# Pooling stage of a two-layer decoder step: small products of the sample outputs placed behind the third gate unit

## The chip, the cores and the metric

The kernel runs on one core of one Trainium2 chip. The metric is the time of one execution on the device in microseconds (us). The engines have in-order programs that meet at semaphores: TensorE (matmuls, which write to PSUM), VectorE, ScalarE, GpSimd, and SyncE (SP), which issues most of the DMAs.

## The reference

One inference step of a decoder trunk with two layers, for a prompt group of 1024 tokens and a sample group of 8 sequences with one new token each, which share all weights. So T = 1032 token columns go through each layer. What matters here:

```
m = pool_mix(v_ext, pos_out)          # 4 groups of 128 channels, windows 2, 4, 8, 16
y = einsum('btgc,gcd->btgd', m, pool_w)            # one 128x128 product for each group
pool = y * pool_scale * silu(gate)                 # gate: 4 groups of x @ w_in
b_pool = pool @ pool_up
b_attn = (o * silu(ag)) @ attn_up                  # o: attention output
sub = (sigmoid(mg_pool) * b_pool + sigmoid(mg_attn) * b_attn) @ w_out
```

For the sample group the attention output is `o = einsum('bthc,chd->bthd', o_lat, w_uv)`, with 8 tokens, 8 heads and a latent of 256.

## The kernel before

Activations lie transposed: channels on the 128 partitions, 1032 tokens along the free dimension. Every large product is a **unit** (lines 604 to 620): a slab of weights of 128 output channels, multiplied as three products of split fp32 numbers (high x high, high x low, low x high), each in three parts of 344 columns. A gate unit has 8 weight tiles, so 72 matmuls; a mix unit has one tile, so 9. A unit writes to one of two sets of three PSUM banks, in turn (bank set 0 and 1, `unit_free[0]` and `unit_free[1]`), and waits until the unit before the last, in the same set, has been read. Weights come by DMA into a ring of four pieces (`RAW`), and GpSimd splits each piece into `WH` and `WL` (lines 512 and 514).

The stage at hand is written out by hand, once for each of the two layers. TensorE (lines 943 to 972) goes through: gate unit 0, a small transpose, gate unit 1, 32 small products for the sample outputs (line 952), four transposes (line 956), mix unit 0, 16 **small products** of the sample outputs with `UVF` (line 963, semaphore `os_done`), gate unit 2, mix unit 1, gate unit 3, mix units 2 and 3, and then the loop of the merge units (line 976), which begins with products of `OGH` and `OGL`.

ScalarE (lines 1296 to 1319) takes its work in this order: copies MXH 0 and 1; evacuation of gate units 0 and 1 (`pool_gate`: a copy to SPGB, line 1282, and a sigmoid to SGB, line 1283, which frees the bank set); PVO and its two DMAs; product copy 0 (PMH); a wait for `os_done` (line 1308); copies MXH 2 and 3; a wait for `s_done`; four copies OGH from OT; evacuation of gate unit 2; product copy 1; evacuation of gate unit 3; product copies 2 and 3.

VectorE (lines 1772 to 1803): pooling means 0 and 1 (`mixed`, line 1722: running sums by doubling, into MXF, which ScalarE copies to MXH and VectorE takes the low part MXL from); the sample weights; `gated(0)`, mean 2, `gated(1)`; OLT from line 952's products; the pooling product 0 (line 1762) and PML (line 1770); a wait for `os_done` (line 1790); OT of the sample columns (line 1794, `s_done`); MXL 2; mean 3; MXL 3; pooling product 1; `gated(2)`, `gated(3)`; pooling products 2 and 3.

GpSimd splits weights throughout. Behind mix unit 1 and the OGH copies it makes four OGL (line 561), two behind the split of mix unit 2's weights and two behind that of mix unit 3's, and then splits the merge units' weights.

Copies of ScalarE are recorded on line 1047, where their helper stands.

Of the kernel before, what the change touches and what calls it, by code (L numbers as in the profile page):

```python
# [93 lines left out]
def slab_of(name, n):  # L94

    return next(s for s, x in enumerate(SLABS) if x[0:2] == (name, n))
# [41 lines left out]
def build(nc, x_all, wstream, pages, page_table, ple, state, ukt, uvf, gains, lng, lnb, table, ident,  # L138
          mask, inv, y_all, lat_p, rope_p, pool_p, lat_s, rope_s, pool_s):
    with ExitStack() as ctx:  # L140
# [201 lines left out]

        BLOCKS = [(h, j) for h in range(2) for j in range(SEQ // P)]
        SECOND = [sum(j >= 4 for _, j in BLOCKS[:n]) for n in range(17)]
        GROUPS = SEQ // P
        O_BANK, FILL_BANK = 5, 2
# [226 lines left out]
        def _(pe):  # L573
# [30 lines left out]
            def unit(l, s, xh, xl, i=0, per=0, between=None):  # L604

                par, kt, tiles = par_of(s), SLABS[s][2], piece_tiles(s)
                pe.wait_ge(unit_free[par], q_of(l, s, i, per) + 1)
                for j in range(SLABS[s][3]):
                    slot, q = piece_of(l, s, j, i, per)
                    pe.wait_ge(w_split[slot], q + 1)  # L610
                    for k in range(tiles * j, tiles * (j + 1)):
                        at = slice((k - tiles * j) * P, (k - tiles * j + 1) * P)
                        for n, (w, x) in enumerate(((WH, xh), (WH, xl), (WL, xh))):
                            for c in range(3):
                                last = nc.tensor.matmul(PS[:, 3 * par + c, 0:CH], w[:, slot, at],  # L615
                                                        x(k)[:, c * CH:(c + 1) * CH], start=(k == 0 and n == 0),
                                                        stop=(k == kt - 1 and n == 2))
                    last.then_inc(w_used[slot], 1)
                    if between is not None:
                        between(j)  # L620

            def rows(tensor, base=0):
                return lambda k: tensor[:, base + k, :]
# [166 lines left out]
            for l in range(DEPTH):  # L790
# [144 lines left out]
                def gate_unit(g):  # L935
                    unit(l, slab_of("pg", g), rows(XH), rows(XL))

                def mix_unit(g):

                    pe.wait_ge(mix_ready, 4 * l + g + 1)  # L940
                    unit(l, slab_of("pw", g), lambda k: MXH[g // 2][:, g % 2, :], lambda k: MXL[g // 2][:, g % 2, :])
# [14 lines left out]
                    last = nc.tensor.transpose(PS[0:23, 6, g * P:(g + 1) * P], PVX[:, g, PAD + T - 23:PAD + T], IDENT[:])  # L956
                last.then_inc(pvt_done, 1)
                mix_unit(0)
                pe.wait_ge(aux_in, 32 * l + 32)
                pe.wait_ge(olt, l + 1)  # L960
                for h in range(PAIRS):
# [2 lines left out]
                                                UVF[:, k, h * P:(h + 1) * P],  # L964
                                                OLT[:, k, 2 * h:2 * h + 2, :], start=(k == 0), stop=(k == KC - 1))
                last.then_inc(os_done, 1)

                gate_unit(2)
                mix_unit(1)
                gate_unit(3)  # L970
                mix_unit(2)
# [476 lines left out]
        def _(dve):  # L1448
# [41 lines left out]
            def x_wait(t):  # L1490
                for i, (lo, _) in enumerate(X_LOADS):
                    if t == lo:
                        dve.wait_ge(x_in[i], 16)
# [31 lines left out]
            for l in range(DEPTH):  # L1525
# [36 lines left out]
                def scaled(part):  # L1562

                    lo, hi = ((0, KC), (KC, KQ + KC))[part]
                    dve.wait_ge(rt_ready, 6 * l + 3 * part + 3)
                    own(v.reciprocal(RT[:, 1 - part, :], RT[:, 1 - part, :]))
                    for _, k in LATENTS[lo:hi]:
                        v.scalar_tensor_tensor(out=CR[:, k, :], in0=CR[:, k, :], scalar=GL[:, k:k + 1], in1=RT[:, 1 - part, :],
                                               op0=ALU.mult, op1=ALU.mult).then_inc(cn_ready, 1)
# [469 lines left out]
```

## Time and profile before

| | us |
|---|---|
| median of 3 runs | 2044.54 |
| lowest and highest | 2037.77, 2045.38 |
| the profiled execution | 2032.2 |
| its span in the trace | 2030.4 |
| TensorE busy | 1912.3 |
| VectorE, GpSimd, ScalarE busy | 905.2, 737.0, 565.4 |
| mean granted clock of TensorE | 0.98 |

The span goes from the first to the last instruction of the profiled execution; 1.8 us of its time lie around it. All starts below are from the span's start. The pooling stage lies at about 575 to 640 us in the first layer and 1567 to 1632 us in the second. The granted clock is a share of full speed: 1.00 is 2.4 GHz and 0.50 is 1.2 GHz. Matmuls overlap, so a unit's time is read from the start of its first matmul to the start of what follows.

### The profile page before, as it was taken

How to read it: one execution, taken by the hardware profiler on the slowest of the kernel's cores; microseconds unless marked ns; L12 is line 12 of the kernel's file. 1: busy time of each engine (PE TensorE's matmuls, PEld its weight loads, DVE VectorE, ACT ScalarE, POOL GpSimd, SP SyncE). 2: the span in 40 equal slices, each digit the busy share in tenths (PEclk: the TensorE clock that was granted, in tenths of full speed). 3: DMA queues.
4: the chain of work that ended last, by engine and by line, in shares of the span. 5: the costliest groups of instructions: out<-in, count | busy, mean ns of one | idle time of the engine just before them, and what ended most of it. 6: DMA issues, size and time to landing. Idle time of an engine off the chain costs nothing.

```text
span 2030.4 us, 31146 instructions
## 1 busy us (share of the span) xinstructions
PE 1912.3 (94%) x12391; PEld 1816.3 (89%) x12391; DVE 905.2 (45%) x1484; ACT 565.4 (28%) x997; POOL 737.0 (36%) x743
## 2 busy tenths in 40 slices
PE   6999899999999999999989989999999999999994
PEld 5998888888799999999989968888878999999994
DVE  4344566664164111535454535666623721134216
ACT  6123444443122010201251334444421310120002
POOL 3332343342145333434244322343312443334434
PEclk9999999999999999999999999999999899999997
DMA  5213221053812221222132141121365122222222
GB/s 212 74 47 131 65 64 62 22 177 123 288 34 62 78 66 56 89 89 68 30 128 55 41 165 33 55 64 61 138 234 181 32 89 72 67 68 87 66 67 84
DMA packets 94746, 183.96 MB, mean 91 GB/s; under 512 B 12086, under 2 KB 35942, under 8 KB 93964
## 3 DMA queue, kind: packets, MB, share of 16 engines
q1 hardware_dynamic: 73440, 135.43, 21.7%
q10 hardware_dynamic: 21180, 46.80, 6.1%
q8 instruction: 85, 1.39, 0.3%
q14 instruction: 41, 0.34, 0.1%
HBM read 150.19 MB, written 32.45 MB: 90 GB/s over the span
## 4 chain that ended last, share of the span: by engine, by line
PE 73%; DVE 11%; ACT 9%; issue 3%; ACTq 1%; DMA 1%; POOL 1%; DVEq 0%; SPq 0%; POOLq 0%
PE PS L615 52%; PE PS L710 5%; PE PS L638 4%; PE PS L595 4%; DVE MX L1662 3%; ACT PB L1243 2%; ACT PTH L1047 2%; DVE PTL L1650 2%; PE PS L695 2%; PE PS L730 1%; PE PS L671 1%; DVE PS L1661 1%; PE PS L754 1%; DMA RAW<-in_wstream 1%; ACT FST L1047 1%
## 5 line engine op out<-in xcount | busy, mean ns | idle before, releaser
L512 POOL CAST WH<-RAW 128x512 fp32r<-128x512 f32 (+3 forms) x292 | 200.7, 687 | 905.8 <-DMA RAW<-in_wstream 905.8
L514 POOL TENSOR_TENSOR WL<-RAW,WH 128x512 fp32r<-128x512 f32 (+3 forms) x292 | 382.2, 1309 | 23.5
L615 PE MATMUL PS<-XH,WH 128*128 128x344 f32 x1344 | 290.0, 324 | 4.6 <-ACT SGB L1283 3.9
L615 PE MATMUL PS<-XL,WH 128*128 128x344 f32 x1344 | 287.4, 322 | 0.0
L615 PE MATMUL PS<-XH,WL 128*128 128x344 f32 x1344 | 286.8, 322 | 0.0
L615 PEld LDWEIGHTS PS<-XH,WH 128*128 128x128 f32 x1344 | 228.0, 190 | 7.3 <-ACT SGB L1283 4.5
L615 PEld LDWEIGHTS PS<-XH,WL 128*128 128x128 f32 x1344 | 227.5, 189 | 0.0
L615 PEld LDWEIGHTS PS<-XL,WH 128*128 128x128 f32 x1344 | 227.3, 190 | 0.0
L533 POOL TENSOR_SCALAR PB<-PB,RC 128x128 f32<-128x128 f32 (+7 forms) x128 | 96.1, 751 | 333.3 <-DVE RC L1644 333.3
L638 PE MATMUL PS<-XH,WH 128*128 128x344 f32 x384 | 127.4, 332 | 29.1 <-ACT FST L1047 29.1
L1243 ACT ACTIVATE PB<-PS,NB 128x128 f32<-128x128 f32 (+7 forms) x128 | 95.0, 742 | 188.2 <-DVE NB L1663 187.9
L1819 DVE TENSOR_TENSOR SGP<-PS,SGP 128x1032 f32<-128x1032 f32 x16 | 19.7, 1233 | 242.1 <-PE PS L615 242.1
L638 PE MATMUL PS<-XL,WH 128*128 128x344 f32 x384 | 124.3, 324 | 0.0
L638 PE MATMUL PS<-XH,WL 128*128 128x344 f32 x384 | 123.6, 322 | 0.0
L638 PEld LDWEIGHTS PS<-XH,WH 128*128 128x128 f32 x384 | 72.6, 189 | 41.1 <-ACT FST L1047 40.4
L1650 DVE TENSOR_TENSOR PTL<-PS,PTH 128x512 fp32r<-128x512 f32 (+3 forms) x128 | 75.8, 592 | 68.9 <-ACT PTH L1047 67.8
L1662 DVE TENSOR_REDUCE MX<-PS 128x1 f32<-128x128 f32 (+7 forms) x128 | 97.0, 758 | 4.4
L1047 ACT ACTIVATE PTH<-PS 128x512 fp32r<-128x512 f32 (+1 forms) x192 | 86.7, 488 | 32.1 <-PE PS L671 30.8
L660 PE MATMUL PS<-KH,QH 128*128 128x512 f32 (+1 forms) x192 | 75.4, 393 | 7.9 <-DVEq L1623 7.9
L695 PE MATMUL PS<-PTH,VSP 128*128 128x256 f32 x320 | 75.5, 272 | 3.6 <-DVE PTL L1654 3.6
L695 PE MATMUL PS<-PTL,VSP 128*128 128x256 f32 x320 | 73.8, 278 | 0.0
L638 PEld LDWEIGHTS PS<-XH,WL 128*128 128x128 f32 x384 | 72.5, 189 | 1.1
(275 smaller groups left out, 3860.2 us busy)
## 6 DMA issues: line engine op xcount, KB each, us to landing
RAW<-in_wstream SPq DMA_DIRECT2D x236, 256.0 KB, 2.7
PAGES<-in_pages SPq DMA_DIRECT2D x128, 320.0 KB, 4.9
spill_p<-PST ACTq DMA_DIRECT2D x16, 516.0 KB, 2.9
spill_g<-FST ACTq DMA_DIRECT2D x48, 172.0 KB, 1.9
SGL<-spill_g ACTq DMA_DIRECT2D x16, 516.0 KB, 4.4
PRJ<-spill_p ACTq DMA_DIRECT2D x16, 516.0 KB, 4.4
spill_v<-VSTG ACTq DMA_DIRECT2D x16, 512.0 KB, 2.8
VSP<-spill_v SPq DMA_DIRECT2D x8, 1024.0 KB, 5.3
```

The source lines that it names most:

```text
L512: pool.tensor_copy(WH[:, slot, 0:size], RAW[:, slot, 0:size]).then_inc(w_high[slot], 1)
L514: pool.tensor_tensor(WL[:, slot, 0:size], RAW[:, slot, 0:size], f(WH[:, slot, 0:size]), ALU.subtract).then_inc(w_split[slot], 1)
L533: pool.tensor_scalar(PB[:, n % 2, 0:keys], PB[:, n % 2, 0:keys], RC[:, n:n + 1], 1.0, ALU.mult, ALU.mult).then_inc(nm_done, 1)
L595: last = nc.tensor.matmul(PS[:, 3 * par + c, 0:w], wt[:, slot, at], x(k)[:, cut[c]], start=(k == 0 and n == 0), stop=(k == kt - 1 and n == 2))
L615: last = nc.tensor.matmul(PS[:, 3 * par + c, 0:CH], w[:, slot, at], x(k)[:, c * CH:(c + 1) * CH], start=(k == 0 and n == 0), stop=(k == kt ...
L638: last = nc.tensor.matmul(PS[:, FILL_BANK, 0:CH], w[:, slot, (k % 4) * P:(k % 4 + 1) * P], x[:, k, c * CH:(c + 1) * CH], start=(step == 0) ...
L695: last = nc.tensor.matmul(PS[:, o_bank(g), lo:2 * P], VSP[:, kb, h * P:(h + 1) * P], pt[:, kb, lo:2 * P], start=(kb == 0 and m == 0), stop ...
L710: last = nc.tensor.matmul(PS[:, PV_BANKS[chunk % 2], 0:CH], w[:, slot, (k % 4) * P:(k % 4 + 1) * P], x[:, k, c * CH:(c + 1) * CH], start=( ...
L1047: return nc.scalar.activation(dst, src, ACT.Copy)
L1243: nc.scalar.activation(PB[:, n % 2, 0:keys], score_banks(n)[:, 0:keys], ACT.Exp, bias=NB[:, n:n + 1], scale=SCALE, accum_out=SUM[:, n:n + ...
L1650: v.tensor_tensor(PTL[:, 0:w, c0:c0 + P], PS[:, 6, 0:w * P].rearrange("p (k c) -> p k c", c=P), f(PTH[:, 0:w, c0:c0 + P]), ALU.subtract).t ...
L1662: own(v.tensor_reduce(MX[:, n:n + 1], row[:, 0:(j + 1) * P], AX_X, ALU.max))
```

## The change

On TensorE, the call of gate unit 2 moves from behind the small products of line 963 to a place ahead of them and of the two waits in front of them. The other engines' programs stay as they are. The order becomes: mix unit 0, gate unit 2, small products, mix unit 1, gate unit 3, mix units 2 and 3.

```
                 last.then_inc(pvt_done, 1)
                 mix_unit(0)
+                gate_unit(2)
                 pe.wait_ge(aux_in, 32 * l + 32)
                 pe.wait_ge(olt, l + 1)
                 for h in range(PAIRS):
...
                 last.then_inc(os_done, 1)
-
-                gate_unit(2)
                 mix_unit(1)
                 gate_unit(3)
                 mix_unit(2)
```

## Rows read from the trace of the kernel before

**Rows 1.** The page: busy time of the engines, and the chain's shares by engine.
```profile
PE 1912.3 (94%) x12391; PEld 1816.3 (89%) x12391; DVE 905.2 (45%) x1484; ACT 565.4 (28%) x997; POOL 737.0 (36%) x743
PE 73%; DVE 11%; ACT 9%; issue 3%; ACTq 1%; DMA 1%; POOL 1%; DVEq 0%; SPq 0%; POOLq 0%
```

**Rows 2.** Waits of TensorE, 590 to 660 us: total, times, longest.
```profile
PE PS L615 <- ACT SGB L1283: 2.0, 1, 2.0
PE PS L615 <- DVEq L1766: 1.1, 1, 1.1
...
```

**Rows 3.** The chain in order of time, first layer: start, duration, what.
```profile
605.52 1.07 ACT MXH L1047
...
606.62 1.87 DVE MXL L1754
...
615.41 0.18 DVE MXF L1742
...
616.58 3.91 ACT OGH L1047 x4
...
```

**Rows 4.** Timeline of TensorE, first layer: start, duration, instructions, idle before.
```profile
583.93 0.75 PE L615 MATMUL PS<-XH,WH 128*128 128x344 f32 x3
...
595.41 3.63 PE L952 MATMUL PS<-SELW,OLS 128*128 128x8 f32 x32
598.90 0.60 PE L956 MATMUL PS<-IDENT,PVX 128*23 128x128 f32 x4
599.25 0.90 PE L615 MATMUL PS<-MXH,WH 128*128 128x344 f32 x3
...
601.92 3.56 PE L963 MATMUL PS<-OLT,UVF 128*128 128x16 f32 x16
605.33 1.21 PE L615 MATMUL PS<-XH,WH 128*128 128x344 f32 x3
...
618.82 0.64 PE L615 MATMUL PS<-MXH,WH 128*128 128x344 f32 x3
...
622.37 0.74 PE L615 MATMUL PS<-XH,WH 128*128 128x344 f32 x3 [1.97 <-ACT SGB L1283]
...
635.38 0.63 PE L615 MATMUL PS<-MXH,WH 128*128 128x344 f32 x3
```

**Rows 5.** The same timeline in the second layer.
```profile
1594.40 3.43 PE L963 MATMUL PS<-OLT,UVF 128*128 128x16 f32 x16
1597.66 1.21 PE L615 MATMUL PS<-XH,WH 128*128 128x344 f32 x3
...
1611.58 0.64 PE L615 MATMUL PS<-MXH,WH 128*128 128x344 f32 x3
...
1615.10 0.74 PE L615 MATMUL PS<-XH,WH 128*128 128x344 f32 x3 [1.93 <-ACT SGB L1283]
...
1626.59 0.63 PE L615 MATMUL PS<-MXH,WH 128*128 128x344 f32 x3
```

**Rows 6.** Windows: stretch, length, TensorE busy, granted clock, DMA share, GB/s.
```profile
605.33:609.77 4.44, 4.44 (x16) 0.50 0.00 0
...
1597.66:1602.97 5.31, 5.31 (x19) 0.50 0.00 0
```

**Rows 7.** Timeline of TensorE at the kernel's start.
```profile
14.16 1.20 PE L615 MATMUL PS<-PLH,WH 128*128 128x344 f32 x3 [6.01 <-POOL WL L514]
...
19.43 0.65 PE L615 MATMUL PS<-PLH,WH 128*128 128x344 f32 x3
```

**Rows 8.** Line 1754 alone: least, median and greatest ns; first and last start.
```profile
L1754 DVE TENSOR_TENSOR MXL<-MXF,MXH x8: 1232/1316/2245, 580.6 to 1609.4; 128x1032 fp32r<-128x1032 f32 x8
```

**Rows 9.** Timeline of VectorE, end of the third pooling mean.
```profile
600.03 0.17 DVE L1742 SCALAR_TENSOR_TENSOR MXF<-RED,PVX 128x8 f32<-128x8 f32 x1
```

**Rows 10.** Timeline of GpSimd: the first OGL pair, and weights behind the last.
```profile
621.84 5.75 POOL L561 TENSOR_TENSOR OGL<-OT,OGH 128x1032 fp32r<-128x1032 f32 x2
...
634.06 0.61 POOL L512 CAST WH<-RAW 128x512 fp32r<-128x512 f32 x1
```

More of the change, by code:

```diff
@@ L958, in _ @@
                 mix_unit(0)
+                gate_unit(2)
                 pe.wait_ge(aux_in, 32 * l + 32)
@@ L966, in _ @@
                 last.then_inc(os_done, 1)
-                gate_unit(2)
                 mix_unit(1)
```

## The prediction

> **What bounds the kernel now.** I read the page's busy shares and its chain of work first. TensorE is busy 94% of the span and holds 73% of the chain, so only two things change the time: work that TensorE does more or less slowly, and moments in which it has nothing to do [rows 1]. Next the waits of TensorE in the stretch around the change: 2.0 us for ScalarE's sigmoid (line 1283, the evacuation of gate unit 2) and 1.1 us for VectorE. The reader should see that the first is a wait of gate unit 3 for the bank set that gate unit 2 filled [rows 2]. Then the chain in order of time, followed back from that wait: gate unit 3 starts at 622.37 us, because ScalarE's two evacuations of gate unit 2 end there; these come after four copies into OGH, these after MXH, this after VectorE's fourth pooling mean (the one with window 16, to 615.6 us), this after MXL, this after another MXH copy at 605.52 us, and this after the small products of line 963 [rows 3]. So everything from 605.5 to 622.4 us, 16.9 us on ScalarE and VectorE, begins with the end of the small products (the semaphore os_done) and ends with the start of gate unit 3. It is no dependence of data for the most part: ScalarE and VectorE each have a wait for os_done in their program (lines 1308 and 1790), and what stands behind it waits too. Last, the timeline of TensorE in both layers: today gate unit 2 and mix unit 1 (13.5 + 1.6 us in layer 0) run under this chain and hide all of it but 2.0 us [rows 2, 4].
>
> **The change, part by part.** No instruction is added or removed. Gate unit 2 (72 matmuls) goes ahead of two waits and 16 small products, in each of the two layers. No DMA is issued by TensorE; SP's loads wait only for pieces that are used no later than before, so nothing is moved past SP's or GpSimd's queue.
>
> *Gate unit 2 starts earlier.* Its bank set is free (its predecessor there, gate unit 1, ends at 595.41 us, and ScalarE needs for such a set the 1.9 us from the OGH copies' end to gate unit 3's start [rows 3, 4]) and its weights are split. So it starts where mix unit 0 ends, about 601.9 and 1594.4 us, 3.4 and 3.3 us earlier [rows 4, 5].
>
> *Its duration.* A gate unit at the full clock takes 595.41 - 583.93 = 11.48 us. Gate unit 2 now takes 618.82 - 605.33 = 13.49 us in layer 0 and 1611.58 - 1597.66 = 13.92 us in layer 1 [rows 4, 5], because the granted clock was 0.50 (the 1.2 GHz level) for its first 4.44 and 5.31 us [rows 6]; 2.0 us lost in 4.44 us, so 0.45 us for each slow us. The clock had fallen after the small products of line 952, and mix unit 0 already ran slowly. It has come back 4.4 to 5.3 us after dense work began: so in rows 6, and also at the kernel's start, where the first unit began at 14.16 us after 6.01 us of idleness and was fast from 19.43 us [rows 6, 7]. With mix unit 0 directly ahead of gate unit 2, dense work begins at 599.3 us, so the clock should be back near 604.2 us, which leaves 1.6 to 2.7 slow us for gate unit 2, about 1.0 us lost: 12.5 us. Bounds: 11.5 us (never slow) and 13.9 us (as slow as today's layer 1).
>
> *The small products.* They take 605.33 - 601.92 = 3.41 us and 1597.66 - 1594.40 = 3.26 us now, at the slow clock. Behind a gate unit they would run at the full one. The nearest row is the 32 products of line 952, also with 128x128 weights and few columns, at the full clock: 598.90 - 595.41 = 3.49 us, 0.109 us each [rows 4], so 16 take 1.75 us. Bounds 1.7 and 3.4 us.
>
> *What waits behind them.* os_done thus comes 12.5 + 1.75 - 3.41 = 10.8 us later in layer 0 and 12.4 + 1.75 - 3.26 = 10.9 us later in layer 1. Queued behind its wait are, on ScalarE, the MXH copies 2 and 3, the OGH copies, the evacuation of gate unit 2 and later ones; on VectorE, the two small products with OT, MXL, the fourth mean and the third and later pooling products. Gate unit 3 waits for that evacuation. The cover that hid 14.9 of the 16.9 us is gone, since gate unit 2 has been done before the chain begins; only mix unit 1 (1.6 us) is left. TensorE then stands idle for some 15 us in each layer where it stands 2.0 us now, and gate unit 3 starts later by the whole delay of os_done. One correction: MXL took 1.87 us in layer 0 while the median of its eight instances is 1.32 us [rows 3, 8]; GpSimd split a piece of weights beside it, which will have been done long before. I take 0.35 us off per layer; bounds 0 and 0.9.
>
> *The clock of gate unit 3.* After such an idle stretch I expect 4.4 to 5.3 slow us as above, 2.2 us lost. Today gate unit 3 loses 635.38 - 622.37 - 11.48 = 1.5 us in layer 0 and nothing in layer 1 (1626.59 - 1615.10 = 11.49 us) [rows 4, 5]. So it costs +0.7 and +2.2 us; bounds for both together -1.5 and +3.3. The rows at hand disagree: an idleness of about 2 us cost the clock in one layer and not in the other. The Trainium skill (TensorE: Matmul & The Clock Gate, Part 1) says that the half rate is the default and that an idle stretch brings it back; by that the fall is certain in both layers, and the bound of -1.5 us would be dropped.
>
> *What is late next.* GpSimd's four OGL subtractions wait for the OGH copies and for mix unit 1; the first began 1.4 us behind the copies' end and GpSimd turned to the next weights at 634.06 us, 1.3 us ahead of gate unit 3's end [rows 3, 4, 10]. They move by the same 10.8 us as gate unit 3, and gate unit 3 gets longer, so the slack stays. The products of VectorE behind gate unit 3, with their 1.1 us wait, move along too. Priced at nothing for that reason; if that cover failed it would cost 1 to 2 us a layer.
>
> *Sum.* Layer 0: 10.8 - 0.35 + 0.7 = 11.2 us. Layer 1: 10.9 - 0.35 + 2.2 = 12.8 us. Together 24 us. The profiled execution took 2032.2 us, so 2056 us by its own measure. The three timed runs have a median of 2044.54 us, 12 us above it; the trace says nothing of where these lie, and none of my terms depends on them, so I add the 24 us to the median: **2068 us**. Ends of the effect: with the low bounds 9.8 + 9.9 - 1.8 - 1.5 = 16 us; with the high ones 13.9 + 13.9 + 3.3 = 31 us.
>
> **The rivals.**
> *Faster: only TensorE's own side counts.* If the two engines could do the work behind their waits for os_done, the chain would start with the third pooling mean, whose MXF is ready at 600.2 us [rows 9], and gate unit 3 would find its banks empty. Then TensorE keeps what it gains: 1.65 us from small products at the full clock, 1.0 to 1.4 us from gate unit 2, and the 2.0 us wait, so 4.8 us a layer, about 2035 us. This decides from the point where the chain behind os_done is shorter than 1.6 us of mix unit 1 plus the wait. Against it: the MXH copy at 605.52 us has had its input for over 5 us and starts right with the end of line 963 [rows 3, 4, 9], so the engine does not go round its wait. The skill says the same as a rule (the same page, Architectural detail): ScalarE and VectorE take their queues strictly in order. It is the rule that speaks against this change, and the trace agrees; if it did not hold, the sum would be the 2035 us just given. On the other side the page advises to keep TensorE's dense work together (Why this matters for your kernels), which the change does for mix unit 0 and gate unit 2; that rule alone would give the first two of these gains, 2.7 to 3 us a layer, and so about 2039 us. Chance of this rival 3%.
> *No difference: the delay is taken up later.* TensorE would have to save some 14 of the 24 us in later waits, 2044 to 2054 us. In this stretch its only two waits of a microsecond or more take 3.1 us together, and both are for work which its own units trigger [rows 2]. Chance 4%.
> *Dearer: the clock stays low for longer.* If the small products behind gate unit 2 run at the slow level, gate unit 2 is slow as today, and gate unit 3 pays in full in both layers, the sum is the upper 31 us: 2076 us. Against it: today the clock is back within 5.3 us of dense work each time. Chance 13%.
>
> **How the numbers follow.** The forecast, 16 to 28 us more (2060 to 2073 us), has 80%. The three runs before spread over 7.6 us, which is added to the bounds: the range is 2056 to 2078 us. A measurement of this kernel tells about 0.5% (10 us) from no change. Slower by more: forecast and the dear rival, 93%; within: 4%; faster by more: 3%.
>
> **What the profile after would show.** Right: the small products of line 963 behind gate unit 2's last matmul, at about 0.11 us each; ScalarE's MXH copy idle until their end; one wait of TensorE of 14 to 16 us for line 1283 in each layer; about 0.50 of the clock at gate unit 3's start in both; from then on the same pattern, 11 and 13 us later. Wrong: that wait under 10 us, or a wait of TensorE for GpSimd behind gate unit 3. The prediction fails if ScalarE's evacuation of gate unit 2 starts before the OGH copies, or if the time is within 10 us of before.

## The result, and the profile after

The changed kernel took 2059.8 us (median of 6 runs, 2053.14 to 2064.57) against 2039.56 us of the kernel before (6 runs, 2035.46 to 2045.38). The ratio is 1.0095, with a 95% interval of 1.007 to 1.0119: about 20 us slower, with an interval of 14 to 24 us. The forecast was 24 us on a median that stood at 2044.54 us then; the time lies inside the forecast range, just below the 2060 to 2073 us that had a chance of 80%; the 20 us lie inside that band's 16 to 28 us. Three executions of the experiments below (8136.73 us of the kernel before, 6168.93 us of the kernel with both reorderings, 3758.59 us of the changed kernel again) lie far above all others of their kernels and are left out of the medians and ratios.

The profiled execution of the changed kernel took 2064.57 us and its span is 2062.8 us. The first view is the waits of TensorE between 590 and 670 us (what waited, for whom: us in total, times, longest). It answers to [rows 2].

```profile
PE PS L615 <- ACT SGB L1282: 14.7, 1, 14.7
PE PS L615 <- DVEq L1765: 1.1, 1, 1.1
PE PS L615 <- issue: 0.7, 1, 0.7
```

One wait has grown from 2.0 to 14.7 us and the others are as before. (One line was removed ahead of them, so lines behind 968 have numbers one lower, and the small products are line 964.) The timeline of TensorE in the first layer answers to [rows 4]: start, duration, instructions, idle before in brackets.

```profile
602.42 3.63 PE L952 MATMUL PS<-SELW,OLS 128*128 128x8 f32 x32
...
606.57 1.21 PE L615 MATMUL PS<-MXH,WH 128*128 128x344 f32 x3
...
609.30 0.67 PE L615 MATMUL PS<-XH,WH 128*128 128x344 f32 x3
...
620.71 1.85 PE L964 MATMUL PS<-OLT,UVF 128*128 128x16 f32 x16
622.41 0.72 PE L615 MATMUL PS<-MXH,WH 128*128 128x344 f32 x3
...
638.81 1.23 PE L615 MATMUL PS<-XH,WH 128*128 128x344 f32 x3 [14.72 <-ACT SGB L1282]
...
652.37 0.63 PE L615 MATMUL PS<-MXH,WH 128*128 128x344 f32 x3
...
657.38 0.74 PE L615 MATMUL PS<-OGH,WH 128*128 128x344 f32 x3 [1.10 <-DVEq L1765]
```

Gate unit 2 starts at 609.30 us, right behind mix unit 0, and takes 11.41 us at the full clock; the small products follow and take 1.70 us; then mix unit 1; then TensorE stands for 14.72 us. The second layer has the same rows: small products at 1627.05 us, gate unit 3 at 1645.14 us behind another 14.72 us of idleness. The granted clock in stretches of the first layer (stretch, length, TensorE busy, granted clock, DMA share, GB/s) answers to [rows 6]:

```profile
606.57:609.30 2.73, 2.73 (x12) 0.50 0.08 17
609.30:620.71 11.41, 11.41 (x73) 1.00 0.16 48
620.71:622.40 1.69, 1.69 (x18) 1.00 0.14 39
...
638.81:643.90 5.09, 5.09 (x19) 0.54 0.00 0
```

Mix unit 0 runs at the slow level, gate unit 2 and the small products at the full one, and gate unit 3 begins slowly.

The chain that ended last shows what these 14.72 us are made of (start, duration, what), and answers to [rows 3].

```profile
622.60 1.08 ACT MXH L1046
...
623.70 1.23 DVE MXL L1753
624.93 1.16 DVE SUMA L1729
...
631.85 0.18 DVE MXF L1741
...
633.02 3.91 ACT OGH L1046 x4
636.92 0.91 ACT SPGB L1046
637.84 0.93 ACT SGB L1282
```

It is the chain of the kernel before, link by link, 17.1 us later by the clock of the trace; 7.3 us of these lie ahead of mix unit 0, where nothing was changed. Counted from mix unit 0's start, the small products end 9.8 us later in the first layer and 10.1 us in the second (said: 10.8 and 10.9). Nothing of TensorE lies beside it any more but mix unit 1.

I compare the kernels by one length in each layer: from the start of mix unit 0 to the start of the merge units' first product (the one with OGH). Before it is 41.2 us (599.25 [rows 4] to 640.40 us) and, by the same rows of the second layer (1591.67 to 1631.60 us), 39.9 us. After it is 50.8 and 51.4 us. Together 21.1 us longer, beside the 20.2 us between the medians. The two profiled executions are 32.4 us apart; the other 11 us lie mostly ahead of the stage (line 952 starts at 602.42 us after 595.41 us, though nothing was changed there) and between the two layers' stages (4 us). In the traces below, line 952 starts at any time from 596.7 to 605.5 us, and repeated runs of one kernel spread by 10 us as well, so I put nothing of it down to the change; what makes it is open.

### The profile page after: what moved, and what is told of

Its sections match the earlier page's. It is cut to its first block, busy times and chain, and to the rows that moved or that the text cites. A ratio compares the mean times of both kernels' runs of the same rounds, so it can differ in the third digit from the quotient of the medians.

```text
span 2062.8 us, 31146 instructions
## 1 busy us (share of the span) xinstructions
PE 1921.0 (93%) x12391; PEld 1825.6 (89%) x12391; DVE 905.1 (44%) x1484; ACT 565.6 (27%) x997; POOL 737.0 (36%) x743
## 4 chain that ended last, share of the span: by engine, by line
PE 74%; DVE 10%; ACT 9%; issue 3%; ACTq 1%; DMA 1%; POOL 1%; DVEq 0%; SPq 0%; POOLq 0%
PE PS L615 52%; PE PS L710 5%; PE PS L638 4%; PE PS L595 4%; DVE MX L1661 3%; ACT PB L1242 2%; ACT PTH L1046 2%; DVE PTL L1649 2%; PE PS L695 2%; PE PS L730 1%; PE PS L671 1%; DVE PS L1660 1%; PE PS L754 1%; DMA RAW<-in_wstream 1%; ACT FST L1046 1%
## 5 line engine op out<-in xcount | busy, mean ns | idle before, releaser
L1046 ACT ACTIVATE PTH<-PS 128x512 fp32r<-128x512 f32 (+1 forms) x192 | 86.8, 488 | 34.9 <-PE PS L671 33.3
```

The lines of the kernel that those rows point to most:

```text
L1046: return nc.scalar.activation(dst, src, ACT.Copy)
```

## The experiments

Times are medians, and a comparison with the kernel before goes by the ratio; each kernel was timed beside the kernel before on the same chip (2037.3 us for the first four experiments, 2035.7 us for the last four).

**The evacuation of gate unit 2 ahead of the wait.** The changed kernel with one line moved on ScalarE.

```
                 product_copy(0)
+                pool_gate(2)
                 act.wait_ge(os_done, l + 1)
...
                     copy(OGH[:, m, :], OT[:, m, :]).then_inc(og_high, 1)
-                pool_gate(2)
                 product_copy(1)
```

> The changed kernel, with one edit on ScalarE: the evacuation of gate unit 2 goes ahead of its wait for os_done. Theory (gate unit 3 waits 14.7 us only because ScalarE's program has that evacuation behind os_done): the wait for line 1283's sigmoid is gone in both layers and gate unit 3 starts right behind mix unit 1. What is late next is behind os_done too: pooling product 1, PML 1 and the four OGL of GpSimd, so the merge units start 9 to 12 us earlier a layer than in the changed kernel and not the full 17: 2036 to 2042 us. Rival (VectorE or GpSimd hold gate unit 3 back as well): a wait of 8 us or more stays ahead of gate unit 3, and the time stays over 2050 us.

Measured: 2045.5 us, ratio to the kernel before 1.0035 (1.0021 to 1.005), so some 12 us of the 20 came back. The timeline of TensorE in the first layer:

```profile
614.90 1.85 PE L964 MATMUL PS<-OLT,UVF 128*128 128x16 f32 x16
616.60 0.71 PE L615 MATMUL PS<-MXH,WH 128*128 128x344 f32 x3
...
618.11 0.63 PE L615 MATMUL PS<-XH,WH 128*128 128x344 f32 x3
...
630.20 0.72 PE L615 MATMUL PS<-MXH,WH 128*128 128x344 f32 x3 [0.55 <-issue]
...
636.57 1.20 PE L615 MATMUL PS<-MXH,WH 128*128 128x344 f32 x3 [4.69 <-ACT SGB L1282]
...
644.46 1.23 PE L615 MATMUL PS<-OGH,WH 128*128 128x344 f32 x3 [4.97 <-POOL WL L514]
```

Gate unit 3 starts at 618.11 us with no wait at all: its wait was ScalarE's order and nothing else. But two others take its place, 4.7 us for the evacuation of gate unit 3 (ScalarE comes to it only behind PML 1, which is behind os_done too) and 5.0 us for weights that GpSimd splits behind its OGL. The stage is 44.0 us long in both layers, 6.8 us in all above the kernel before. The wait went as the theory said, but the merge units start 6.9 and 7.4 us earlier than in the changed kernel and not 9 to 12, so the time of 2036 to 2042 us was set too low. The miss is on GpSimd (timeline, first layer):

```profile
628.56 4.78 POOL L561 TENSOR_TENSOR OGL<-OT,OGH 128x1032 fp32r<-128x1032 f32 x2 [10.60 <-ACT OGH L1046]
...
635.94 5.69 POOL L561 TENSOR_TENSOR OGL<-OT,OGH 128x1032 fp32r<-128x1032 f32 x2
...
642.27 2.13 POOL L514 TENSOR_TENSOR WL<-RAW,WH 128x512 fp32r<-128x512 f32 x1
```

From the first OGL to the end of the split at 644.4 us GpSimd is never idle for more than 0.1 us, so its 15.8 us of work behind the first OGH copy set the start of the merge units, and the 4.7 us wait lies beside it. The OGH copies come behind the fourth mean, which this run left where it was.

**The fourth mean ahead of the wait.** The changed kernel with an edit on VectorE alone.

```
                 mixed_product(0)
+                mixed(3, POOL_WINDOWS[3])
                 dve.wait_ge(os_done, l + 1)
...
                 mix_low(2)
-                mixed(3, POOL_WINDOWS[3])
                 mix_low(3)
```

> The changed kernel with one edit on VectorE: the fourth pooling mean goes ahead of the wait for os_done; ScalarE's order stays. Theory: the chain behind os_done loses the mean's 7.2 us and one semaphore step (two MXH copies, four OGH copies, the evacuation: about 8 us are left), so TensorE's wait ahead of gate unit 3 falls from 14.7 to 6 to 7 us and the time by about 16 us, to 2042 to 2046 us. Rival (the mean is not on the chain, ScalarE's copies alone set it): the wait stays over 12 us and the time over 2055 us.

Measured: 2039.4 us, ratio 1.0009 (0.9993 to 1.0026). The wait ahead of gate unit 3 (TensorE, first layer):

```profile
623.58 0.72 PE L615 MATMUL PS<-MXH,WH 128*128 128x344 f32 x3
...
631.48 1.23 PE L615 MATMUL PS<-XH,WH 128*128 128x344 f32 x3 [6.23 <-ACT SGB L1282]
```

From os_done to gate unit 3 it is 7.9 us now and 16.4 us in the changed kernel, in both layers. The link removed was worth 8.5 us, and the wait is in the expected 6 to 7 us. The time is below the expected 2042 to 2046 us. By the stage's length (43.0 and 42.9 us) the kernel should stand 4.8 us above the one before; it was timed 1.8 us above it, with an interval that ends at 5.3 us.

**Both.** The two edits together on the changed kernel.

> As the run before, and on VectorE the fourth pooling mean (7.2 us) goes ahead of its wait for os_done too. Theory (all of the cost is order behind the two waits): nothing holds TensorE for long in this stage; the merge units start 17 us a layer earlier than in the changed kernel, so 2024 to 2030 us, some 12 us less than the kernel before. Rival (moving the small products costs by itself, through the clock or through contention of VectorE and GpSimd): not below the kernel before, 2036 us or more.

Measured: 2026.4 us, ratio 0.9941 (0.992 to 0.9963): 12 us faster than the kernel before and some 31 us faster than the changed one, with TensorE's order as the change has it. The stage is 34.9 us long in both layers. TensorE, first layer:

```profile
626.96 0.63 PE L615 MATMUL PS<-XH,WH 128*128 128x344 f32 x3
...
638.34 0.63 PE L615 MATMUL PS<-MXH,WH 128*128 128x344 f32 x3
...
640.59 0.72 PE L615 MATMUL PS<-MXH,WH 128*128 128x344 f32 x3 [0.68 <-issue]
...
644.27 0.74 PE L615 MATMUL PS<-OGH,WH 128*128 128x344 f32 x3 [2.01 <-POOL WL L514]
```

The rival, that the new place of the small products costs by itself, is out: its whole cost was what waited behind them. The 2.0 us wait that is left is GpSimd's, busy from the first OGL on, as with the evacuation alone.

**Half the way.** The small products in the middle of gate unit 2.

```
-                gate_unit(2)
...
+                def small_products(j):
...
+                    if j == 1:
+                        return
...
+                unit(l, slab_of("pg", 2), rows(XH), rows(XL), between=small_products)
```

> The changed kernel with the small products in the middle of gate unit 2 (behind its first 36 matmuls). A dose of half: os_done comes about 5.7 us earlier than in the changed kernel. Theory (gate unit 3 starts a fixed 16.4 us behind os_done): TensorE's wait ahead of gate unit 3 is 14.7 - 5.7 = 9.0 us, and the time is about 11 us below the changed kernel, 2046 to 2051 us. Rival (the cost is in the order of mix unit 0 and gate unit 2, or in the clock): no proportion, the time within 4 us of one of the two kernels.

Measured: 2055.0 us, ratio 1.0077 (1.0051 to 1.0104). TensorE's wait is 10.8 us in both layers; I expected 9.0 us, and a time of 2046 to 2051 us. By its interval the time can't be told from the changed kernel's; the stages (47.3 and 47.7 us) are 7.1 us shorter in all. The cause of the longer wait is on VectorE (timeline, first layer; start and duration):

```profile
619.49 1.65 DVE L1758 TENSOR_TENSOR MXL<-MXF,MXH 128x1032 fp32r<-128x1032 f32 x1 [0.71 <-ACT MXH L1051]
621.06 2.32 DVE L1734 TENSOR_TENSOR SUMA<-PVX 128x1039 f32<-128x1039 f32 x1
623.42 1.24 DVE L1734 TENSOR_TENSOR SUMB<-SUMA 128x1037 f32<-128x1037 f32 x1
```

and GpSimd beside it:

```profile
620.13 2.15 POOL L514 TENSOR_TENSOR WL<-RAW,WH 128x512 fp32r<-128x512 f32 x1
```

MXL and the first running sum took 1.65 and 2.32 us, where the changed kernel has 1.23 us for each, and they lie across GpSimd's split of gate unit 3's second piece (2.15 us where it mostly takes 1.3). The second layer has the same three durations within 0.01 us. The chain from os_done to gate unit 3 is 18.2 us here and not 16.4, and these two operations are 1.5 us of the 1.8. So the dose has its effect, os_done 4.6 and 5.7 us earlier (counted from mix unit 0) against a wait 3.9 us shorter; the chain that it releases is no constant, it depends on what GpSimd does beside it. The Trainium skill (SBUF — State Buffer, Who interferes with whom) says that a VectorE operation with two inputs in SBUF and a GpSimd operation that reads SBUF take turns for whole instructions. The first sum and MXL have two such inputs, GpSimd's split reads SBUF, and the rows agree: the split ends at 622.28 us, and the sum at 623.38 us, about its usual time later. That the two pieces coincide is read from the times, no run took GpSimd's split away.

**TensorE kept busy.** The changed kernel with products that nobody reads in the idle stretch.

```
                 mix_unit(1)
+                pe.wait_ge(pvt_evac, l + 1)
+                pe.sem_inc(spare, 1)
+                for n in range(92):
+                    nc.tensor.matmul(PS[:, 6, 0:CH], XH[:, 0, 0:P], XH[:, 1 + n % 7, 0:CH], start=True, stop=True)
                 gate_unit(3)
```

> The changed kernel with 92 products of 128x344 that nobody reads, between mix unit 1 and gate unit 3, about 14.5 us at the full clock: TensorE idles hardly at all, but gate unit 3 still starts when its bank set is free. Theory (of the cost, 2.1 + 2.4 us is gate unit 3 running at the slow clock behind the idle stretch): gate unit 3 takes 11.5 us in place of 13.6 and 13.9 us, and the time is 2 to 5 us below the changed kernel, all of the rest of the cost remaining. Rival (the slow clock has another cause than the idleness): gate unit 3 takes over 13 us and the time is that of the changed kernel.

Measured: 2054.0 us, ratio 1.0089 (1.0058 to 1.0119), beside the changed kernel's 2057.1 us on the same chip. TensorE, first layer:

```profile
620.38 14.71 PE L972 MATMUL PS<-XH 128*128 128x344 f32 x92
635.29 0.74 PE L615 MATMUL PS<-XH,WH 128*128 128x344 f32 x3 [0.19 <-ACT SGB L1286]
...
646.78 0.63 PE L615 MATMUL PS<-MXH,WH 128*128 128x344 f32 x3
```

Gate unit 3 takes 646.78 - 635.29 = 11.49 us, and 11.49 us in the second layer, where the changed kernel takes 13.56 and 13.85 us. This shows the term of the slow clock: 2.1 and 2.4 us, and that the idleness brings it. The stage is 3.6 us shorter in all than the changed kernel's, the medians 3.1 us apart; the intervals of the two ratios overlap, so in time alone it isn't shown.

**The changed kernel again.**

> The changed kernel again, as it is, beside the three kernels that follow. Expected: 18 to 22 us over the kernel before, a wait of 14.7 us ahead of gate unit 3 in both layers. If the difference comes out under 14 us, the 21 us of the stage's lengths in the two traces are not the whole account.

Measured: 2057.1 us, ratio 1.0095 (1.0066 to 1.0125), as in the first measurement. The expected wait was not read again.

**The mean ahead of the wait, in the kernel before.** The same edit on VectorE as above, with TensorE's order of before.

> The kernel before, its TensorE order untouched, with the fourth pooling mean ahead of VectorE's wait for os_done: how much of the gain of the reordered kernels can be had without moving the small products. Here the evacuation of gate unit 2 can't start before that unit ends, so only the 2.0 us wait of gate unit 3 and its slow clock in the first layer can go. Theory (the move itself is worth the faster clock of small products and gate unit 2): 2 to 5 us below the kernel before, and so 6 us or more above the kernel with both reorderings. Rival (the reordering alone brings the gain, the move nothing): 10 us or more below the kernel before.

Measured: 2032.4 us, ratio 0.9976 (0.9956 to 0.9995). So the reordering on VectorE alone brings 1 to 9 us. The two layers differ (TensorE):

```profile
605.71 1.89 PE L963 MATMUL PS<-OLT,UVF 128*128 128x16 f32 x16
607.45 0.72 PE L615 MATMUL PS<-XH,WH 128*128 128x344 f32 x3
...
618.92 0.64 PE L615 MATMUL PS<-MXH,WH 128*128 128x344 f32 x3
...
626.08 1.23 PE L615 MATMUL PS<-XH,WH 128*128 128x344 f32 x3 [5.58 <-ACT SGB L1283]
...
1616.96 0.74 PE L615 MATMUL PS<-XH,WH 128*128 128x344 f32 x3 [0.69 <-ACT SGB L1283]
```

In the second layer the 1.93 us wait falls to 0.69 us, but the merge units' wait grows from 1.10 to 2.11 us. In the first the clock was back early in this execution: small products and gate unit 2 took 1.74 and 11.47 us in place of 3.41 and 13.49 us. The chain is no shorter for it and ran to 626.0 us. In both layers the small products end before VectorE comes to the fourth mean, which now stands ahead of OT. So OT, the OGH copies and the evacuation wait for the mean (609.53 to 619.29 us in the first layer, with running sums of 1.65 and 2.21 us) and no longer for os_done, and gate unit 3 waited for 5.58 us. What TensorE wins there turns into waiting. The two stages are 80.3 us in all, 0.8 us less than before, against 69.9 us with both edits and the small products moved. The expected 2 to 5 us were met by the time, but by the stage's rows only 0.8 us of it lie here; the rest stays open. The stages' lengths and the ratios (0.9941 against 0.9976, with intervals that overlap a little) speak for the move being worth something once the queues are in order. They don't show it: the kernel with both edits also has ScalarE's evacuation ahead of the OGH copies. The kernel before with that evacuation ahead of the OGH copies too was not run, so part of the 12 us may be had without the move.

**OGH ahead of MXH.** One more edit, on the kernel with both: ScalarE makes the four OGH copies first.

```
+                act.wait_ge(s_done, l + 1)
+                for m in range(PAIRS):
+                    copy(OGH[:, m, :], OT[:, m, :]).then_inc(og_high, 1)
                 mix_copy(2)
                 mix_copy(3)
-                act.wait_ge(s_done, l + 1)
...
```

> The kernel with both reorderings (evacuation of gate unit 2 and fourth mean ahead of the waits), with one more edit on ScalarE: the four OGH copies go ahead of MXH copies 2 and 3. There the merge units waited 2.0 us a layer for weights that GpSimd splits behind its OGL. Theory (GpSimd's OGL start with the OGH copies, so they and the weights come 1.9 us earlier): that wait is gone or under 0.5 us, and the time is 2 to 4 us below that kernel, some 14 us below the kernel before. Rival (the MXH copies, now 3.9 us later, become late for mix units 2 and 3, or VectorE's products do): a wait of 2 us or more elsewhere in the stage, no gain.

Measured: 2025.6 us, ratio 0.9942 (0.992 to 0.9963), the same as without the edit. The rival held: the wait for GpSimd's weights is gone, and one for VectorE of 2.46 us stands in its place. TensorE, then VectorE, first layer:

```profile
635.89 0.74 PE L615 MATMUL PS<-OGH,WH 128*128 128x344 f32 x3 [2.46 <-DVEq L1765]
```

```profile
622.22 3.43 DVE L1753 TENSOR_TENSOR MXL<-MXF,MXH 128x1032 fp32r<-128x1032 f32 x2 [5.01 <-ACT MXH L1046]
...
629.37 4.99 DVE L1748 TENSOR_TENSOR SPGB<-SPGB,SGB 128x1032 f32<-128x1032 f32 x2
```

Two gating products took 4.99 us beside GpSimd's OGL, where one alone takes 1.23 us. The stage is 35.35 us long in both layers, beside 34.9 us. The two orders are equal in time, and either is the best version found: about 11 us below the kernel before.

## Why the prediction was right or wrong

- **The mechanism** held in each link. The only new wait is that of gate unit 3 for line 1282, 14.7 us in both layers (said: 14 to 16 us), and taking either link from behind os_done takes it away or shortens it by that link. The rival in which ScalarE works on past its wait is out: its MXH copy, whose input was ready at 607 us, starts with the end of the small products, after 10.7 us in which the engine was idle (ScalarE, changed kernel).

```profile
622.60 1.07 ACT L1046 ACTIVATE MXH<-MXF 128x1032 fp32r<-128x1032 f32 x1 [10.67 <-PE PS L964]
```

- **Gate unit 2** took 11.4 and 11.9 us, said 12.5 and 12.4 us. The step that was off is the return of the clock: 1.6 to 2.7 slow us were left for this unit, but it had none in the first layer and about 1 in the second. I took dense work as beginning with mix unit 0 and a return 4.4 to 5.3 us later; it came 2.7 and some 3.7 us later. This is the largest part of the error, 1.6 us, and in part chance: in the later traces with the same three steps on TensorE, gate unit 2 took 11.8 to 12.4 us.
- **The small products** took 1.70 us in both layers, said 1.75 us.
- **The chain behind os_done** took 16.4 us in both layers. It was 17.0 and 17.4 us (from line 963's end to gate unit 3), so the correction was 0.6 and 1.1 us and not 0.35 us: MXL took 1.23 us, its least value rather than its median, and in the second layer it had taken 2.25 us before (the greatest of [rows 8]), which the forecast did not price apart from the first layer's 1.87 us.
- **Gate unit 3's clock** cost +0.55 and +2.4 us, said +0.7 and +2.2 us. The rule of the Trainium skill (TensorE: Matmul & The Clock Gate, Part 1), that idleness brings the half rate back, held in both layers after 14.7 us, and the run with TensorE kept busy shows the cause.
- **What is late next**: GpSimd's OGL ended 7.0 us ahead of gate unit 3 (645.4 against 652.4 us), so that cover held. The slack was said to stay at 1.3 us and grew, since the OGL no longer begin behind a split of weights. SP's loads were argued wrongly, since by the forecast itself gate unit 3's pieces are used later; it cost nothing, as no wait of TensorE for weights followed in the stage.
- **The sum** was 24 us; the stages say 21.1 us and the medians 20.2 us. The forecast time was 8 us too high: 5 us because the kernel before stands at 2039.6 us over six runs and stood at 2044.5 us over the first three, 3 us from these terms; the rest, under 1 us, is within the noise.
- **The other rivals**: the dear one is out, as the small products ran at the full clock and gate unit 2 was not slow for long. So is the one in which the delay is taken up later: behind gate unit 3, TensorE's waits in the stage are 0.7 and 1.1 us as before, and the time is 20 us longer.
- One sentence was too wide: that the waits for os_done are "no dependence of data for the most part". That holds for the evacuation and the mean, as the runs show. The OGH copies read OT, whose sample columns come from the small products. The MXH copies 2 and 3 do need os_done too, because MXH's second buffer lies over UVF (lines 207 and 220 of the kernel before), which the small products read; for that reason no run had them ahead of the wait.

## What to carry to other kernels

A small step that one engine makes for others is placed by what stands behind the wait for its result in their programs, not by its own time: 16 products of 1.7 us held back 16 us of ScalarE's and VectorE's work. Before a producer is moved later, list everything queued behind its consumers' waits, and move what doesn't need the result ahead of them; with that done, the kernel with the same move was 12 us faster than the one before instead of 20 us slower (how much of it is the move's own was not shown). A cover counts only while it lies beside the chain: the 12 us unit that had hidden it was still there, in front of it.

## What the runs showed of the hardware

The same instruction of VectorE with two inputs in SBUF takes 1.23 us alone and up to 3.4 us beside GpSimd; in the changed kernel:

```profile
606.92 1.23 DVE L1748 TENSOR_TENSOR SPGB<-SPGB,SGB 128x1032 f32<-128x1032 f32 x1
...
643.06 3.44 DVE L1748 TENSOR_TENSOR SPGB<-SPGB,SGB 128x1032 f32<-128x1032 f32 x1
```

and GpSimd beside the second of them (it was idle during the first):

```profile
639.66 5.74 POOL L561 TENSOR_TENSOR OGL<-OT,OGH 128x1032 fp32r<-128x1032 f32 x2
```

so a chain moved in time meets other work of GpSimd and changes its length, by 1.8 us in the run with half the way. And 14.7 us of products whose results nobody reads, in a gap that TensorE had anyway, spared 2.1 to 2.4 us of the unit that followed.
